# Triple mixer: the gate product as stacked fp32r behind the latent projections, decays summed by scans, decayed keys transposed between two parts of a projection piece

## The reference

```python
z = h @ w_in[l]
(na_q, na_k, na_v, gq, gk, gv, gr, gfl, gbl, c_q, c_kv, k_rope, gates) = split_cols_2(z, IN_SPLITS)
g_f = jax.nn.log_sigmoid((gfl @ gla_gf_up[l] + gla_gf_bias[l])) / GLA_GATE_TAU      # gfl: 16 wide, tau 16
g_b = jax.nn.log_sigmoid((gbl @ gla_gb_up[l] + gla_gb_bias[l])) / GLA_GATE_TAU
...
def gla_chunked(q, k, v, g, strict):       # chunks of 64 tokens; once forward, once on the reversed sequence
    b = jnp.cumsum(g, axis=3)              # running sum of the log decays within a chunk
    b_last = b[:, :, :, -1:, :]
    qe = q * jnp.exp(b)
    ke = k * jnp.exp(-b)
    k_end = k * jnp.exp(b_last - b)        # what a key adds to the state behind its chunk
    a = jnp.where(tri, jnp.einsum('bhnid,bhnjd->bhnij', qe, ke), 0.0)
    upd = jnp.einsum('bhncd,bhncv->bhndv', k_end, v)
```

## Time and profile before

| | |
|---|---|
| median of three runs | 2318.72 us (2318.62 to 2319.46) |
| the profiled execution's own time | 2319.0 us |
| its span, first to last instruction | 2317.1 us |
| PE busy | 2307.1 us, 100% |
| PE weight loads | 2019.2 us, 87% |
| DVE busy | 1682.3 us, 73% |
| ACT busy | 1256.1 us, 54% |
| DMA | 409.51 MB, mean 177 GB/s |
| mean granted clock of TensorE | 0.999 of full speed |
| triple mixer of layer 0 | about 1243 to 1478 us of the span |
| triple mixer of layer 1 | about 1870 to 2105 us |

### The profile page before, as it was taken

How to read it: one execution, slowest core, us unless ns; L and a number is a source line. 1 busy time by engine, 2 the same in 40 slices (tenths; PEclk the granted TensorE clock), 3 DMA queues, 4 the chain that set the end, 5 groups by cost and what they waited for, 6 DMA issues and landing times.

```text
span 2317.1 us, 32714 instructions
## 1 busy us (share of the span) xinstructions
PE 2307.1 (100%) x13658; PEld 2019.2 (87%) x13658; DVE 1682.3 (73%) x2141; ACT 1256.1 (54%) x1523; POOL 79.0 (3%) x116
## 2 busy tenths in 40 slices
PE   9999999999999999999999999999999999999999
PEld 8889889888888978888888878888888888788887
DVE  8867846876876789768766777587687677776873
ACT  6545664554554565545555764455455467554552
POOL 2000000000000020100010000001000100000000
PEclk9999999999999999999999999999999999999999
DMA  7655435555555525655655534566556555344554
GB/s 228 195 186 178 136 138 195 186 185 186 193 191 183 169 75 189 217 188 189 197 185 181 182 128 146 167 196 210 188 189 194 183 184 169 127 149 161 197 183 145
DMA packets 335042, 409.51 MB, mean 177 GB/s; under 512 B 7894, under 2 KB 285104, under 8 KB 334896
## 3 DMA queue, kind: packets, MB, share of 16 engines
q1 hardware_dynamic: 331632, 401.66, 52.6%
q0 software_dynamic: 3072, 5.69, 0.9%
q10 hardware_dynamic: 192, 0.08, 0.0%
HBM read 406.35 MB, written 1.05 MB: 176 GB/s over the span
## 4 chain that ended last, share of the span: by engine, by line
PE 93%; DVE 4%; DMA 1%; ACT 1%; issue 0%; SPq 0%; DVEq 0%; ACTq 0%
PE bank L614 13%; PE acc L614 12%; PE bank L1384 11%; PE bank L622 7%; PE acc L622 6%; PE acc L706 6%; PE bank L706 6%; PE acc L693 4%; PE bank L713 3%; PE acc L713 3%; PE acc L790 3%; PE acc L2772 2%; PE acc L1554 2%; DVE part_lo L504 1%; PE bank L3349 1%; PE bank L652 1%
## 5 line engine op out<-in xcount | busy, mean ns | idle before, releaser
L504 DVE TENSOR_TENSOR part_lo<-raw,part_hi 128x2048 fp32r<-128x2048 f32 (+3 forms) x390 | 870.4, 2235 | 342.2 <-ACT part_hi L497 338.8
L497 ACT ACTIVATE part_hi<-raw 128x2048 fp32r<-128x2048 f32 (+3 forms) x390 | 728.3, 1868 | 331.6 <-DMA raw<-in_ffn_w 98.9
L614 PE MATMUL bank<-hT,part_hi 128*128 128x512 f32 x1408 | 328.2, 390 | 0.0
L614 PEld LDWEIGHTS bank<-hT,part_hi 128*128 128x128 f32 x1408 | 261.6, 188 | 52.9 <-ACT part_hi L497 0.2
L614 PE MATMUL acc<-hT,part_hi 128*128 128x512 f32 x1280 | 298.2, 390 | 0.0
L614 PEld LDWEIGHTS acc<-hT,part_hi 128*128 128x128 f32 x1280 | 237.7, 188 | 47.7
L1384 PE MATMUL bank<-part_hi,hT 128*128 128x512 f32 x768 | 247.4, 395 | 0.0
L622 PE MATMUL bank<-hT,part_lo 128*128 128x256 f32 x1408 | 184.2, 284 | 0.0
L622 PEld LDWEIGHTS bank<-hT,part_lo 128*128 128x128 f32 x1408 | 178.1, 192 | 3.6
L1384 PEld LDWEIGHTS bank<-part_hi,hT 128*128 128x128 f32 x768 | 144.2, 188 | 31.2 <-issue 1.7
L622 PE MATMUL acc<-hT,part_lo 128*128 128x256 f32 x1280 | 166.4, 283 | 0.2 <-DVE part_lo L504 0.2
(11 more groups left out here) (547 smaller groups left out, 3274.3 us busy)
## 6 DMA issues: line engine op xcount, KB each, us to landing
raw<-in_ffn_w SPq DMA_DIRECT2D x122, 1024.0 KB, 5.2
raw<-in_w_in SPq DMA_DIRECT2D x48, 1024.0 KB, 4.9
raw<-in_ffn_w_up SPq DMA_DIRECT2D x44, 1024.0 KB, 5.2
raw<-in_ffn_w_gate SPq DMA_DIRECT2D x43, 1024.0 KB, 5.2
raw<-in_ffn_w_down SPq DMA_DIRECT2D x32, 1024.0 KB, 5.2
raw<-in_hy_w_in SPq DMA_DIRECT2D x22, 1024.0 KB, 4.9
raw<-in_ffn_w_down SPq DMA_DIRECT2D x16, 768.0 KB, 4.4
raw<-in_ffn_w SPq DMA_DIRECT2D x12, 768.0 KB, 4.5
```

The source lines that it names most:

```text
L497: t.e.activation(part_hi[:, n % SLOTS, 0:size], raw[:, n % SLOTS, 0:size], ACT.Copy).then_inc(hi_ready, 1)
L504: t.e.tensor_tensor(part_lo[:, n % SLOTS, 0:size], raw[:, n % SLOTS, 0:size], part_hi[:, n % SLOTS, 0:size].bitcast(F32), ALU.subtract).th ...
L614: mm = pe.matmul(tiles[:, f, :].rearrange("p (h s) -> p h s", h=2), slot_cols(s, 0)[:, k, f * P:(f + 1) * P], hT[:, :, k, :], start=(first ...
```

## The change

It has four parts, all in the triple mixers of both layers.

- **Gate product.** It becomes four fp32r products of 96 rows, with channels stationary and tokens moving, so that its output has channels in the partitions. Three bands of rows give the three passes: `glx` holds the inputs' high halves, their low halves in rows 32 to 47, the high halves again in rows 64 to 79, and ones; `gate_s` holds the weights' high halves twice and their low halves in rows 64 to 80. Two memsets of DVE clear both (`gate_room`), ACT copies into `gate_s` twice (`gate_hi`) and into `glx` twice (`gl_flipped`), DVE makes a subtraction for each (`gl_low`). The product moves from ahead of the latent projections to behind them.
- **Running sums.** DVE's minimum and subtraction move ahead to the flips of `lkT`, and four scans of 256 elements follow there, restarted by a 0/1 row (`C_CHUNK`) at chunk borders, backward ones by reading in reverse. `gsum` holds the sums, channels in the partitions. The 0/1 products on PE go.
- **Decays to the chunk's end.** DVE subtracts the sums from the chunk's whole (`kf`), ACT takes the exponential in steps 4 and 6, DVE multiplies by the keys in steps 6 and 8, PE transposes the result to tokens in the partitions in step 9 (two groups of four), and ACT copies it out as `ke`. `ep` and `em` are made from `gsum` in ACT's steps 8 and 10. DVE's two multiplies in `grow` go.
- **The last piece's parts** lie in steps 8 and 10 instead of 9 and 10.

```diff
     same = i // GLA_C == j // GLA_C
-    for at, m in ((C_LE, i <= j), (C_GT, i > j), (C_GE, i >= j), (C_LT, i < j)):
+    for at, m in ((C_LE, i <= j), (C_GT, i > j)):
         c[:, at:at + P] = same & m
...
+                if i == 9:
+                    for d in range(2):
+                        pe.wait_ge(gla_kf, t.see(gla_kf))
+                        b = claim(t)
                         for a in range(TT):
-                            mm = pe.matmul(bank[:, b, j * S + a * P:j * S + (a + 1) * P], gg[:, d, a, j * P:(j + 1) * P],
-                                           late(incl, P), start=True, stop=True)
-                    mm.then_inc(full[b], 1)
-                    b = claim(t)
-                    for a in range(TT):
-                        mm = pe.matmul(bank[:, b, a * 256:(a + 1) * 256], late(rest, P), gg[:, d, a, :],
-                                       start=True, stop=True)
-                    mm.then_inc(full[b], 1)
+                            for j in range(2):
+                                o = (2 * a + j) * P
+                                mm = pe.transpose(bank[:, b, o:o + P], kf[:, d, j * S + a * P:j * S + (a + 1) * P], ident)
+                        mm.then_inc(full[b], 1)
+                        ke_made.append(evicted(t, b))
                 if i in (3, 7):
                     pair = claim_pair(t)
                 if i in NA_PIECES:
                     pair_tensor(t, pair, 1 if i in (1, 5) else 0)
-                if i == 9:
+                if i == 8:
                     last = arrived(t)
-                if i >= 9:
-                    pair_tensor(t, pair, 1, last, (i - 9,))
+                if i in (8, 10):
...
+                if i in (4, 6):
+                    d = i // 2 - 2
+                    act.wait_ge(gla_sums, l + 1)
+                    act.activation(kf[:, d, :], kf[:, d, :], ACT.Exp, scale=tau).then_inc(gla_kexp, 1)
+                if i in (8, 10):
+                    d = i // 2 - 4
+                    sums_of = gsum[:, d, :].rearrange("p (j s) -> p j s", j=2)
+                    act.activation(ep[:, d, :, :], sums_of, ACT.Exp, scale=tau)
+                    act.activation(em[:, d, :, :], sums_of, ACT.Exp, scale=-tau).then_inc(gla_exp, 1)
+                if i == 9:
+                    ke_out(0)
+                    ke_out(1)
...
                 if i in (6, 8):
-                    t.banks.take(), t.banks.take()
+                    d = i // 2 - 3
+                    dve.wait_ge(gla_kexp, t.see(gla_kexp))
+                    v = kf[:, d, :].rearrange("p (j s) -> p j s", j=2)
+                    dve.tensor_tensor(v, v, gkT[:, :, :], ALU.mult).then_inc(gla_kf, 1)
+                if i in (8, 10):
+                    t.banks.take()
...
-            for b in range(4):
-                dve.wait_ge(*evicted(t, b))
-            for d in range(2):
-                ins = dve.tensor_tensor(ke[:, d, :, :], ke[:, d, :, :], z[:, :, Z_GK:Z_GK + 256], ALU.mult)
-            ins.then_inc(gla_ke, 1)
+            dve.wait_ge(gla_exp, t.see(gla_exp, 2))
...
             pe = t.e
-            pe.wait_ge(gla_ke, t.see(gla_ke))
             for d in range(2):
+                pe.wait_ge(*ke_made[d])
...
-            pe.wait_ge(gl_flipped, t.see(gl_flipped))
-            for d in range(2):
-                for a in range(TT):
-                    mm = pe.matmul(acc[:, 2 + d, a * 256:(a + 1) * 256], gl_rows[:, d, a * P:(a + 1) * P], gate_up[:, d, :],
-                                   start=True, stop=True)
-            mm.then_inc(gl_in, 1)
...
+            pe.wait_ge(gl_low, t.see(gl_low))
+            for d in range(2):
+                for j in range(2):
+                    mm = pe.matmul(acc[:, 2 + d, j * S:(j + 1) * S], gate_s[:, d, j * P:(j + 1) * P], glx[:, d, :],
+                                   start=True, stop=True)
+            mm.then_inc(gl_in, 1)
...
+            act.wait_ge(later_in, later_loaded(l))
+            act.wait_ge(gate_room, l + 1)
+            act.activation(gate_s[32:48, :, :], gate_up[0:16, :, :], ACT.Copy)
+            act.activation(gate_s[0:17, :, :], gate_up[0:17, :, :], ACT.Copy).then_inc(gate_hi, 1)
             pair = take_pair(t)
             next_hi(t)
             split_flip_scalar(t, brT, 4, lambda k: c_gain(l, k))
             act.wait_ge(gl_flip, t.see(gl_flip))
-            act.activation(glT[:, :, :], acc[0:16, 1, :].rearrange("p (d s) -> p d s", d=2), ACT.Copy)\
-                .then_inc(gl_flipped, 1)
+            gl = acc[0:16, 1, :].rearrange("p (d s) -> p d s", d=2)
+            act.activation(glx[64:80, :, :], gl, ACT.Copy)
+            act.activation(glx[0:16, :, :], gl, ACT.Copy).then_inc(gl_flipped, 1)
...
+            dve.memset(glx[:, :, :].bitcast(F32), 1.0)
+            dve.memset(gate_s[:, :, :].bitcast(F32), 0.0).then_inc(gate_room, 1)
             dve.wait_ge(c_squares, t.see(c_squares))
             root_vector(t, stat[:, 0, 24:28], 256)
             dve.sem_inc(c_roots, 1)
             nq_made = [evicted(t, b) for b in take_pair(t)]
             next_lo(t)
+            dve.wait_ge(gate_hi, l + 1)
+            dve.tensor_tensor(gate_s[64:81, :, :], gate_up[0:17, :, :], gate_s[0:17, :, :].bitcast(F32), ALU.subtract)
             split_flip_vector(t, brT, 4, lambda k: c_gain(l, k), signal=False)
+            dve.wait_ge(gl_flipped, t.see(gl_flipped))
+            dve.tensor_tensor(glx[32:48, :, :], acc[0:16, 1, :].rearrange("p (d s) -> p d s", d=2),
+                              glx[0:16, :, :].bitcast(F32), ALU.subtract).then_inc(gl_low, 1)
...
+            dve.wait_ge(gl_log, t.see(gl_log))
+            for d in range(2):
+                ins = dve.scalar_tensor_tensor(ge[:, d, :], g_raw[:, d, :], 0.0, ge[:, d, :], ALU.min, ALU.subtract)
+            t.done(ins, gl_decays)
+            restart = late(C_CHUNK, S)
+            for d in range(2):
+                for j in range(2):
+                    g_of, sum_of = (v[:, d, j * S:(j + 1) * S] for v in (ge, gsum))
+                    if d:
+                        g_of, sum_of = g_of[:, ::-1], sum_of[:, ::-1]
+                    ins = dve.tensor_tensor_scan(sum_of, restart, g_of, 0.0, ALU.mult, ALU.add)
+            t.link(ins)
...
-            dve.wait_ge(gl_log, t.see(gl_log))
             for d in range(2):
-                ins = dve.scalar_tensor_tensor(gg[:, d, :, :], g_raw[:, d, :, :], 0.0, ge[:, d, :, :], ALU.min,
-                                               ALU.subtract)
-            ins.then_inc(gl_decays, 1)
+                of_chunks = gsum[:, d, :].rearrange("p (n s) -> p n s", s=GLA_C)
+                whole = of_chunks[:, :, (GLA_C - 1, 0)[d]:(GLA_C, 1)[d]].to_broadcast([P, 2 * S // GLA_C, GLA_C])
+                ins = dve.tensor_tensor(kf[:, d, :].rearrange("p (n s) -> p n s", s=GLA_C), whole, of_chunks, ALU.subtract)
+            ins.then_inc(gla_sums, 1)
```

71 lines of the change are left out of this document (30 added, 41 removed).

## The result

The changed kernel takes 2324.61 us (median of 16 runs, 2322.25 to 2325.50), the kernel before 2319.48 us (16 runs, 2318.62 to 2321.11). The ratio is 1.0021, 95% interval 1.0014 to 1.0027: slower by 5.1 us, where 1.5 us had been forecast. The profiled executions took 2324.42 and 2319.0 us, their spans are 2322.6 and 2317.1 us, so the traces show nearly the same step: 5.5 us.

The account below looks back on a forecast made before the run. PE's own work was taken to set the time. Its 4.30 us a layer of freed slots were lost to stalls: 0.65 + 0.1 = 0.75 us a layer, 1.5 us for two, 2320.2 us; own range 2318 to 2322 us.

Parts of the forecast that it names:

- first place: Ahead of the latent projections: delayed ACT and DVE work stalls PE, 0.65 us a layer lost instead of 1.44 us won.
- PE's own work: Gate product and running sums on PE become cheaper products and transposes: 4.30 us a layer relieved, 8.6 us in all.
- Rival (e): Gate product: the stacked fp32r product isn't cheaper than the fp32 one, 2.9 us above the forecast, 2323 us; 4%.
- covered the making of their operand: Ahead of the latent projections: the old gate product, 1.92 us, was said to cover the making of their operand brT.
- The other two waits: Amid the latent products, PE waits for banks that ACT empties: stalls of 0.75 us and 0.4 us more.
- Scans and subtractions in DVE's gap: DVE's idle 4.92 us takes the moved pair and four scans, together 3.9 us, hidden; kf subtractions cost nothing.
- Second place: End of the neighborhood attention: PE stands 2.9 us at the second four transposes, 0.1 us a layer lost instead of 2.86 won.
- Rival (c): Behind the 2.9 us wait the clock falls to 1.2 GHz: 2.7 us a layer, 5.4 us in all, 2325.6 us; 8%.
- Nothing changes outside the two triple mixers: Rest of the kernel: claimed to stay as it was, adding nothing to the sum.
- rival (a): Both places: PE meets no wait, so 8.6 us less, 2310.1 us; 10%.

Follow-up runs that it names:

- e7: Kernel before the change, with only its old gate product moved behind the latent products: 2320.51 us, ratio 1.0005 to the kernel before.
- e1: Changed kernel with ACT's gate_s copies behind the latents' split and flip, and DVE's gate_s subtraction behind its half of that flip: 2322.45 us, ratio 1.0011 to before.
- e2: e1 with both clears (glx, gate_s) at the start of the mixer's DVE program and both subtractions behind the rotation tables: 2320.52 us, ratio 1.0006 to before.
- e6: e5 with DVE making the rotation tables between its second and third low part, ahead of the latents' flip: 2311.12 us, ratio 0.9965 to before.
- e3: Changed kernel with DVE multiplying the decayed keys of direction 1 ahead of its low part in step 7, not in step 8: 2319.33 us, ratio 1.0002 to before.
- e4: Changed kernel with the edits of e2 and e3 together: 2314.90 us, ratio 0.9980 to the kernel before.
- e8: e2 with DVE clearing 1024 unread columns of squares ahead of its direction 1 multiply, to lengthen the 2.7 us wait: 2323.53 us, ratio 1.0016 to before.
- e5: e4 with ACT's direction 0 exponentials in step 9 ahead of its evictions of the decayed keys, not in step 8: 2312.56 us, ratio 0.9972 to before.

## Why the prediction was wrong

Forecast were 2320.2 us, 1.5 us more than before and too little to measure; it came to 2324.61 us, 5.1 us more than before. Of the 4.4 us between forecast and measurement 0.8 are the kernel before, which took 2319.48 us here and 2318.72 in the forecast. The other 3.6 us come from two terms: the first place, which was sized at 0.65 us a layer and took 1.63, and the slow products behind the wait of the second, which the sum had at nothing and the runs at 1.6 us. Point by point:

- **PE's own work**: right. 4.30 us a layer were to leave, 7 to 9 us of busy time in all; 7.1 us did. Both traces have slow products in them, the changed kernel's behind the new wait, the old one's in another mixer (last section). The gate product is 0.48 us as said. Rival (e) is out.
- **First place, +0.65 us a layer: the term that failed most.** The table shows 1.63 us, beyond even the bound of 1.3. The chain was the right one, each link of it is in the trace, but nearly every link was sized too small. Against the prediction's instants, shifted by the 0.75 us of this execution: `gate_room` comes 0.2 us later (the first clear starts 0.14 us late, and the two take 1.02 us where 0.97 was taken), and ACT takes 0.1 us to start on it; the two copies take 1.18 us from the first's start to the next instruction where 1.0 was taken; the low part to the subtraction 2.33 us in place of 2.21; the subtraction, the flip and the handing over to PE 0.1 us more between them. Together PE waits 1.61 us by the list, not 0.95. The other two waits were sized well by the list: 0.74 for 0.75, 0.35 for 0.4. But the list counts a wait from the end of the last product, its drain included. From start to start PE loses a little more: 1.68 us at the first (1271.50 against 1269.82, where the next product would have started), and at the second 0.90 us and then 0.11 us more before the product behind it. These are the last 0.3 us.
- **Its explanation was wrong in one point as well.** The prediction says that the gate product "covered the making of their operand". Its own rows speak against that: `brT` was whole at 1266.84 + 1.65 = 1268.49, and PE came free at 1269.06. e7 shows the same, with half a microsecond to spare, and e1 and e2 show that the wait comes from the work put ahead of that making, in the queues of ACT and DVE. With that work in place, the old product's 1.92 us would have hidden most or all of the 1.6 us; that is an estimate from these rows, and no run has both. The bounds were drawn from how long the new operations are; the answer lay in where they stand.
- **Scans and subtractions in DVE's gap, nothing**: right. Timeline of the changed kernel, DVE, in what was the gap of 4.92 us:

```profile
1316.22 2.44 DVE L3679 TENSOR_TENSOR_SCAN mix<-later_const,gated_room 128x256 f32<-128x256 f32 x4
1320.10 2.29 DVE L507 TENSOR_TENSOR part_lo<-raw,part_hi 128x2048 fp32r<-128x2048 f32 x1 [1.44 <-ACT part_hi L500]
```

  Four scans of 0.67 us (0.65 was taken), and 1.44 us of the gap are left.
- **Second place, a wait of 2.9 us and +0.1 us a layer**: right in layer 1: the wait is 2.70 us and the net 0.10 us. In layer 0 the same wait cost 1.58 us more, for slow products behind it: the term that the sum had at nothing.
- **Rival (c), given 8%**, is that difference, in one layer of two and with less of it: it took all twelve products as slow in both layers, 2.7 us each; the clock came back after 3.5 us, and 1.6 us were lost, once. The Trainium skill (TensorE: Matmul & The Clock Gate, Part 1) says that the half rate is the default and that an idle stretch brings it back. The trace agrees for the fall in layer 0 (0.50 in three windows behind a wait of 2.7 us); in layer 1 the same wait brought no fall, so the stall alone doesn't decide it, and what does is open. The prediction treated the fall as a case for both layers or none; with a weight of a half on each layer it would have been a term of +0.8 us a layer in the sum, not a rival.
- **What (c) rested on**: a mean clock of 0.999 and no wait above 1.3 us, from which it took that what a longer wait does "isn't shown". But the mean hides a fall. In the same trace, in the sparse attention mixer, the granted clock was 0.50 from 827.21, inside the second of two waits of 1.35 and 0.99 us, to 834.03 us. So the trace did show that waits shorter than the 2.9 us that were forecast can have a fall behind them. Timeline and a window of the kernel before:

```profile
826.15 0.52 PE L2311 MATMUL bank<-const,sa_prob 128*128 128x128 f32 x3 [1.35 <-DVE sa_prob L2661]
827.66 0.90 PE L2311 MATMUL bank<-const,sa_prob 128*128 128x128 f32 x3 [0.99 <-DVE sa_prob L2661]
```

```profile
828.00:829.00 1.00, 1.00 (x7) 0.67 (x7) 0.66 (x5) 0.96 (x5) 0.00 (x0) 0.50 0.00 0
```

- **"Nothing changes outside the two triple mixers"**: right to what the runs can tell, with the 0.75 us that come and go.

So the sum should have been 1.63 + 0.1 in each layer, and 1.6 for a fall in one: 5.1 us. The forecast had 1.5. Of the error of 3.6 us, 2.0 are the first place and 1.6 the clock.

Of the two prices of the change e6 pays next to nothing: it is 8.4 us below the kernel before, which is rival (a) (8.6 us), with the same arithmetic as the change on every engine and in another order.

## What to carry to other kernels

When small operations are put into the queue of an engine that feeds PE, ask first what stands behind them in that queue and who waits for it; an operation of half a microsecond whose result is wanted more than ten microseconds later belongs behind the work that is wanted next, and a wait ahead of a long high part costs the whole chain. After each wait that is removed, look for the one that takes its place (here 2.7, then 1.2, then 0.2 us at the end of the neighborhood attention), since it again may be a matter of order. A stall of PE of the length seen here, 2.7 us, should be priced with a share of slow products behind it, even where its own net cost is nothing because it only fills freed slots. And look through the trace before for stretches of lower clock, by windows around its waits, since a mean of 0.999 over the span had such a stretch of 6.8 us in it.

## What the runs showed of the hardware that was not expected

The granted clock behind a wait isn't a matter of the wait alone. At the end of the neighborhood attention, in the profiled executions, two layers each, it fell behind none of the four waits of 1.2 us (e3, e4), behind three of the six waits of 2.7 us (layer 0 of the changed kernel and of e1, layer 1 of e2) and behind both of 3.7 us (e8). Windows of e1, where it fell in layer 0, and of e2, where it fell in layer 1, behind equal waits:

```profile
1376.00:1377.00 1.00, 1.00 (x6) 1.00 (x6) 0.00 (x0) 0.35 (x1) 0.00 (x0) 0.50 0.06 16
```

```profile
2001.00:2002.00 1.00, 1.00 (x7) 1.00 (x6) 0.00 (x0) 0.24 (x1) 0.00 (x0) 0.50 0.00 0
```

A fall there cost 1.3 to 2.4 us. In the sparse attention mixer all ten traces have the same two waits, of 1.35 to 1.38 us and of 0.98 to 0.99 us. Behind them the clock fell in seven (before, e1, e2, e3, e5, e6, e7; for 3.4 or 6.8 us) and stayed at 1.00 in three (the changed kernel, e4, e8). These three are the ones with the wait of 1.4 us for ACT that was the fifth row of the changed kernel's list. Timeline of the changed kernel:

```profile
833.55 0.52 PE L2314 MATMUL bank<-const,sa_prob 128*128 128x128 f32 x3 [1.42 <-ACT gated_room L2490]
```

With slow products PE comes there later and waits less: from the transposes at L1244 (L1247) to the last stretch of products at L693 (L696) the kernel before took 18.32 us with a fall of 6.8 us, the changed kernel 17.78 us with none, and e2 17.75 us with one of 3.4 us. So what a fall costs depends on what stands behind it: 1.3 us and more where only products follow, 0.0 to 0.9 us where PE would have waited anyway.

The changed kernel's sixteen times fit a fall in most runs: fourteen lie between 2324.08 and 2325.50 us, two at 2322.25 and 2322.49, about a fall less. That these two had none behind the new waits is an inference; only one execution of each kernel was profiled, and the mean clock of these two, 0.999, is also that of seven of the others.
